# Joining the two moving operands of a split-precision product: 512 columns into one PSUM bank, halves added on VectorE

## What is computed

```
h = rms_norm(x, mix_norm_pre);  proj = h @ w_in          # then sparse attention, pooling, gating
x = x + rms_norm(mix @ w_out, mix_norm_post)
q = rms_norm(x) @ w_mq;  k = mem_n @ w_mk;  v = mem_n @ w_mv
x = x + rms_norm(attention(q, k, v) @ w_mo, mem_norm_post)
a = causal_conv3(rms_norm(x) @ w_up);  gate, val = split(a)
x = x + rms_norm((gelu(gate) * val) @ w_down, ffn_norm_post)
# second block, on 272 tokens: short-conv mixer, then mLSTM
q, k, v, o, z, g = split(u @ mlstm_in_w);  q = q * DK ** -0.5
out = rms_norm(x)[:, 16:]
```

## Time and profile before

| | us |
|---|---|
| median of 3 runs | 1003.33 (1000.75, 1003.33, 1003.83) |
| profiled execution, its own time | 1002.0 |
| its span, first to last instruction | 1000.3 |
| PE busy | 968.0 (97%), 7853 matmuls |
| VectorE busy | 676.6 (68%) |
| ScalarE busy | 545.8 (55%) |
| GpSimd busy | 135.0 (13%) |
| mean granted TensorE clock | 0.993 of full |

### The profile page before, as it was taken

How to read it: one execution, slowest core, us unless ns; L and a number is a source line. 1 busy time by engine, 2 the same in 40 slices (tenths; PEclk the granted TensorE clock), 3 DMA queues, 4 the chain that set the end, 5 groups by cost and what they waited for, 6 DMA issues and landing times. The chain is left out here.

```text
span 1000.3 us, 20837 instructions
## 1 busy us (share of the span) xinstructions
PE 968.0 (97%) x7853; PEld 928.2 (93%) x7853; DVE 676.6 (68%) x1048; ACT 545.8 (55%) x839; POOL 135.0 (13%) x137
## 2 busy tenths in 40 slices
PE   8998989999999999999999999999999999999997
PEld 7897769999899999998999999999999989999886
DVE  4878765654589988545877777766576447668843
ACT  6468456645499976554444434444453426654633
POOL 3003001001034455000111111101010000000000
PEclk9999989999999999999999999999999999999999
DMA  7743325435346655763455555555555433234551
GB/s 280 244 144 126 106 64 169 148 106 169 106 143 193 189 189 168 232 201 116 147 168 170 175 180 171 176 179 175 161 172 189 146 127 126 89 130 163 189 172 61
DMA packets 45176, 159.06 MB, mean 159 GB/s; under 512 B 6035, under 2 KB 7059, under 8 KB 44860
## 3 DMA queue, kind: packets, MB, share of 16 engines
q1 hardware_dynamic: 44668, 156.61, 48.9%
q0 software_dynamic: 448, 1.59, 0.6%
HBM read 157.11 MB, written 1.06 MB: 158 GB/s over the span
## 5 line engine op out<-in xcount | busy, mean ns | idle before, releaser
L1517 DVE TENSOR_TENSOR w_lo<-raw,w_hi 128x1024 fp32r<-128x1024 f32 x290 | 357.6, 1239 | 141.3 <-ACT w_hi L547 141.0
L547 ACT ACTIVATE w_hi<-raw 128x1024 fp32r<-128x1024 f32 x290 | 304.8, 1054 | 118.6 <-PE acc L1030 85.6
L1028 PE MATMUL acc<-AH,w_hi 128*128 128x256 f32 (+1 forms) x832 | 239.2, 287 | 0.9 <-DVE AL L1538 0.9
L1030 PE MATMUL acc<-AH,w_lo 128*128 128x256 f32 (+1 forms) x832 | 236.6, 284 | 0.0
L1029 PE MATMUL acc<-AL,w_hi 128*128 128x256 f32 (+1 forms) x832 | 236.4, 284 | 0.0
L1028 PE MATMUL acc<-XH,w_hi 128*128 128x256 f32 (+1 forms) x672 | 194.8, 290 | 8.7 <-DVE XL L1543 3.1
L1030 PE MATMUL acc<-XH,w_lo 128*128 128x256 f32 (+1 forms) x672 | 191.4, 285 | 0.0
L1029 PE MATMUL acc<-XL,w_hi 128*128 128x256 f32 (+1 forms) x672 | 191.2, 284 | 0.0
L1028 PEld LDWEIGHTS acc<-AH,w_hi 128*128 128x128 f32 x832 | 158.0, 190 | 2.7 <-issue 1.1
L1030 PEld LDWEIGHTS acc<-AH,w_lo 128*128 128x128 f32 x832 | 157.9, 190 | 0.0
L1029 PEld LDWEIGHTS acc<-AL,w_hi 128*128 128x128 f32 x832 | 157.7, 190 | 0.1
(11 more groups left out here) (357 smaller groups left out, 1404.1 us busy)
## 6 DMA issues: line engine op xcount, KB each, us to landing
raw<-weights SPq DMA_DIRECT2D x290, 512.0 KB, 3.5
cst<-params SPq DMA_DIRECT2D x1, 1195.0 KB, 13.4
XR<-x_t SPq DMA_DIRECT2D x2, 512.0 KB, 4.6
Y<-mem_t SPq DMA_DIRECT2D x1, 1024.0 KB, 10.8
AR<-bias_rows POOLq DMA_DIRECT2D x1, 1024.0 KB, 10.4
out<-AR SPq DMA_DIRECT2D x2, 512.0 KB, 3.0
AR<-final_gain POOLq DMA_DIRECT2D x1, 512.0 KB, 3.7
AR<-onehot SPq DMA_DIRECT2D x1, 66.0 KB
```

The costliest lines, as they stand in the source:

```text
L547: nc.scalar.activation(w_hi[:, n % SLOTS, :], raw[:, n % SLOTS, :], ACT.Copy).then_inc(hi_ready, 1)
L1028: nc.tensor.matmul(o, wh, h, start=start, stop=False)
L1030: return nc.tensor.matmul(o, wl, h, start=False, stop=stop)
L1517: V.tensor_tensor(w_lo[:, s, :], raw[:, s, :], w_hi[:, s, :].bitcast(F32), ALU.subtract).then_inc(lo_ready, 1)
```

## The change

High and low activations are laid into one tensor each (X2, M2, A2), so that one access pattern of 2 x 256 elements reads both. A new routine, `joined`, replaces `chunk`: per block one matmul of 512 moving columns (high and low) with w_hi into a whole bank, and one of 256 columns (high) with w_lo into its first half. It is used for all `mk` chunks, for tiles 0 to 6 of `w_out`, `mo` and `down`, for tiles 1 to 7 of `mq`, and for all of `lq`. The halves are added at evacuation by VectorE (`add_halves`, a reduction of 512 columns to 256). In `w_out`, `mo` and `down` the sum goes to Y, and ScalarE then waits for the evacuation, squares Y and scales it in place. GpSimd waits for `y_squared` in place of the evacuation. In `mq` a second instruction scales the sum, and the bank counts as free only after it. The factor S ** -0.5 moves from the evacuation of `lq` to that of `lk`.

```
-                    wait_chunk(act, n)
-                    nc.scalar.activation(Y[:, m, META:T], acc(t)[:, 0:S], ACT.Copy, scale=col(gain, m)).then_inc(y_ready, 1)
-                    freed(nc.scalar.activation(SQ[:, m, META:T], acc(t)[:, 0:S], ACT.Square), t)
+                    wait_evacuated(act, t)
+                    nc.scalar.activation(SQ[:, m, META:T], Y[:, m, META:T], ACT.Square).then_inc(y_squared, 1)
+                    nc.scalar.activation(Y[:, m, META:T], Y[:, m, META:T], ACT.Copy, scale=col(gain, m)).then_inc(y_ready, 1)
...
+            def joined(n, t, both, k0=0, nk=KT, total=KT, ready=None, order=None):
+                begin(n, t, k0 == 0)
+                o = acc(t)[:, :]
...
+                    nc.tensor.matmul(o.rearrange("p (a b) -> p a b", a=2), w_hi[:, s, cols], both(k),
+                                     start=(k0 == 0 and k == order[0]), stop=False)
+                    last = nc.tensor.matmul(o[:, 0:S], w_lo[:, s, cols], both(k)[:, 0, :], start=False,
+                                            stop=(k0 + nk == total and k == order[-1]))
+                last.then_inc(chunk_done, 1)
...
             for m in range(KT):
-                chunk(CHUNK["w_out"] + m, TILE["w_out"] + m, a_hi, a_lo, S, ready=mix_ready if m == 0 else None,
-                      order=(0, 1, 2, 4, 5, 6, 7, 3) if m == 0 else None)
+                if m < KT - 1:
+                    joined(CHUNK["w_out"] + m, TILE["w_out"] + m, a_parts, ready=mix_ready if m == 0 else None,
+                           order=(0, 1, 2, 4, 5, 6, 7, 3) if m == 0 else None)
+                else:
+                    chunk(CHUNK["w_out"] + m, TILE["w_out"] + m, a_hi, a_lo, S)
...
+            def add_halves(out, t):
+                return V.tensor_reduce(out, acc(t)[:, :].rearrange("p (a b) -> p b a", a=2), AX.X, ALU.add)
+
+            def join_y(name, m, n):
+                if m < KT - 1:
+                    wait_chunk(dve, n)
+                    freed(add_halves(Y[:, m, META:T], TILE[name] + m), TILE[name] + m)
...
-                        freed(V.tensor_copy(KTm[:, c, :], acc(t)[:, 0:S]), t)
+                        freed(add_halves(KTm[:, c, :], t), t)
...
             for m in range(KT):
                 ahead(CHUNK["w_out"] + m)
+                join_y("w_out", m, CHUNK["w_out"] + m)
...
-                freed(V.scalar_tensor_tensor(out=qM[:, m, :], in0=acc(t)[:, 0:S], scalar=(D // MEM_HEADS) ** -0.5, in1=rstd[:, META:T],
+                src = acc(t)[:, 0:S]
+                if m:
+                    src = qM[:, m, :]
+                    chain.link(add_halves(src, t))
+                freed(V.scalar_tensor_tensor(out=qM[:, m, :], in0=src, scalar=(D // MEM_HEADS) ** -0.5, in1=rstd[:, META:T],
...
             for c in range(24):
                 ahead(CHUNK["down"] + c)
+                if c % 3 == 2:
+                    join_y("down", c // 3, CHUNK["down"] + c)
...
-                freed(V.tensor_scalar(lq[:, m, :], acc(t)[:, 0:S], S ** -0.5, None, ALU.mult), t)
+                freed(add_halves(lq[:, m, :], t), t)
```

More of the change, by code:

```diff
@@ L137, in build @@
         XR = sb("XR", [P, KT, T])
[L138 to L143, removed]
+        X2 = sb("X2", [P, 2, KT, T], F32R)
+        M2 = sb("M2", [P, 2, KT, S], F32R)
+        A2 = sb("A2", [P, 2, E_TILES * T], F32R)
+        XH, XL = X2[:, 0, :, :], X2[:, 1, :, :]
+        MH, ML = M2[:, 0, :, :], M2[:, 1, :, :]
+        AH, AL = A2[:, 0, :], A2[:, 1, :]
         cst = sb("cst", [P, NCOLS])
@@ L299, in build @@
         rstd_ready = sem("rstd_ready")
-        y_ready, x_updated = sem("y_ready"), sem("x_updated")
+        y_ready, x_updated, y_squared = sem("y_ready"), sem("x_updated"), sem("y_squared")
         act_ready, act_hi, act_lo = sem("act_ready"), sem("act_hi"), sem("act_lo")
@@ L511, in _ @@
                         ffn_pool(p, 0, ffn_hi(p), ffn_lo(p))
-                sum_squares(lambda m: wait_evacuated(pool, TILE[name] + m), META)
+                sum_squares(lambda m: pool.wait_ge(y_squared, 7 * update + m + 1), META)
             with pool.Fori(0, E_TILES) as i:
@@ L1055, in chunk, with x_parts, m_parts, a_parts @@
                 last.then_inc(chunk_done, 1)
+            def joined(n, t, both, k0=0, nk=KT, total=KT, ready=None, order=None):
+                begin(n, t, k0 == 0)
+                o = acc(t)[:, :]
+                order = order or range(k0, k0 + nk)
+                s = n % SLOTS
+                for k in order:
+                    cols = slice((k - k0) * P, (k - k0 + 1) * P)
+                    if ready:
+                        ready(k)
+                    nc.tensor.matmul(o.rearrange("p (a b) -> p a b", a=2), w_hi[:, s, cols], both(k),
[3 more added lines that the diff above has]
+                last.then_inc(chunk_done, 1)
+            def x_parts(k):
+                return X2[:, :, k, META:T]
+            def m_parts(k):
+                return M2[:, :, k, :]
+            def a_parts(k):
+                return A2[:, :, span(k, S)]
+            def ffn_parts(k):
+                return a_parts(k) if k < 16 else m_parts(k - 16)
+            def l_parts(k):
+                return A2[:, :, (8 + k) * T + META:(9 + k) * T]
             def slots(part, n, cols):
@@ L1254, in _, with step_chunk @@
                     name, c = (("sgu_u", 0), ("pool", 0), ("mk", 0), ("mk", 2), ("mk", 4), ("mk", 6))[h - 1]
-                    x = (mem_h, mem_l) if name == "mk" else (xh, xl)
+                    def step_chunk(i):
+                        if name == "mk":
+                            joined(CHUNK[name] + c + i, TILE[name] + c + i, m_parts)
+                        else:
+                            chunk(CHUNK[name] + c + i, TILE[name] + c + i, xh, xl, S)
                     if h == 1:
@@ L1265, in _ @@
                         pe.wait_ge(mem_lo, 1)
-                    chunk(CHUNK[name] + c, TILE[name] + c, *x, S)
+                    step_chunk(0)
                     pv(h - 1)
-                    chunk(CHUNK[name] + c + 1, TILE[name] + c + 1, *x, S)
+                    step_chunk(1)
                 else:
@@ L1328, in _ @@
             for m in range(KT):
-                chunk(CHUNK["mq"] + m, TILE["mq"] + m, xh, xl, S, ready=raw_ready(RAW_X1) if m == 0 else None,
-                      between=(lambda: spread_rstd(NORM_X1, S)) if m == 0 else None)
+                if m == 0:
+                    chunk(CHUNK["mq"] + m, TILE["mq"] + m, xh, xl, S, ready=raw_ready(RAW_X1), between=lambda: spread_rstd(NORM_X1, S))
+                else:
+                    joined(CHUNK["mq"] + m, TILE["mq"] + m, x_parts)
                 if m == 2:
@@ L1350, in _ @@
             for m in range(KT):
-                chunk(CHUNK["mo"] + m, TILE["mo"] + m, a_hi, a_lo, S,
-                      ready=(lambda k: pe.wait_ge(act_lo, ACT_MEM + k // 2 + 1)) if m == 0 else None)
+                if m < KT - 1:
+                    joined(CHUNK["mo"] + m, TILE["mo"] + m, a_parts,
+                           ready=(lambda k: pe.wait_ge(act_lo, ACT_MEM + k // 2 + 1)) if m == 0 else None)
+                else:
+                    chunk(CHUNK["mo"] + m, TILE["mo"] + m, a_hi, a_lo, S)
             stat_y(NORM_MEMOUT, 2)
@@ L1368, in _ @@
                 for c in range(3):
-                    chunk(CHUNK["down"] + 3 * m + c, TILE["down"] + m, ffn_hi, ffn_lo, S, k0=8 * c,
-                          nk=min(8, FFN_TILES - 8 * c), total=FFN_TILES,
-                          ready=(lambda k: pe.wait_ge(act_lo, ACT_FFN + k + 1)) if m == 0 else None)
+                    n, t, nk = CHUNK["down"] + 3 * m + c, TILE["down"] + m, min(8, FFN_TILES - 8 * c)
+                    if m < KT - 1:
+                        joined(n, t, ffn_parts, 8 * c, nk, FFN_TILES,
+                               (lambda k: pe.wait_ge(act_lo, ACT_FFN + k + 1)) if m == 0 else None)
+                    else:
+                        chunk(n, t, ffn_hi, ffn_lo, S, k0=8 * c, nk=nk, total=FFN_TILES)
             stat_y(NORM_FFN, 3)
@@ L1395, in _ @@
             for m in range(KT):
-                chunk(CHUNK["lq"] + m, TILE["lq"] + m, l_in(AH, META), l_in(AL, META), S, ready=h1_ready if m == 0 else None)
+                joined(CHUNK["lq"] + m, TILE["lq"] + m, l_parts, ready=h1_ready if m == 0 else None)
                 if m == 5:
@@ L1870, in _ @@
                 ahead(CHUNK["mo"] + m)
+                join_y("mo", m, CHUNK["mo"] + m)
             post_norm(NORM_MEMOUT, 1, "g_ffn_pre", META)
@@ L1974, in lk_tiles @@
                     wait_chunk(dve, n)
-                    freed(V.tensor_tensor(lk[:, m, :], acc(t)[:, 0:T], rstd[:, :], ALU.mult), t)
+                    freed(V.scalar_tensor_tensor(out=lk[:, m, :], in0=acc(t)[:, 0:T], scalar=S ** -0.5, in1=rstd[:, :],
+                                                 op0=ALU.mult, op1=ALU.mult), t)
                     apply_norm(PRE_H1, "g_mlstm", 0, rstd[:, :], l_in(AH, 0), l_in(AL, 0), m)
```

2 lines of the change are left out of this document (added).

## The result

The changed kernel took **1014.36 us** (median of 4 runs, 1014.28 to 1014.59) against 1002.64 us of the kernel before (1000.75 to 1003.83, the three runs and the profiled execution together): ratio 1.0119, 95% interval 1.0102 to 1.0137. The forecast was slower, at 1010.1 us (1003 to 1015.5). The profiled execution took 1014.42 us, its span is 1012.7.

A forecast was written before the change was run, and what follows sets the result against it. The kernel was taken as bound by TensorE's matmul pace. Delays of 4.5, 4.3, 0.85, 0.35 and 0.06 less savings of 1.32, 0.55, 0.48 and 0.14 gave +7.6 us on 1002.0, thus 1009.6; forecast median 1010.1 us, range 1003 to 1015.5.

The forecast's parts named there:

- The loop: In w_out and mo, VectorE and ScalarE wait for each other, 3.67 us a turn against TensorE's 2.81: +4.5 and +4.3 us.
- The clock: Rival: the clock falls to half in the longer wait before stat_y, one or two stretches, 1012 to 1013.5 us; 15%.
- `mq`: Stage mq: 56 joined blocks save 0.48 us, the later end adds 0.85 us, net +0.4 us.
- the 0.85: At the end of mq, VectorE's reduction, link and scaling replace one 0.43 us instruction: +0.85 us.
- That is hidden in tiles 1 to 6, since banks are asked for a tile later: In mq, VectorE's longer evacuation of tiles 1 to 6 was to cost nothing; only the end would pay.
- the 0.0086 us: Saving per joined block, 0.3594 us before and 0.3508 after; 450 blocks, 3.9 us at most.
- `lq` and `lk`: Two reductions in lq's gate chain on VectorE, less slack: +0.35 us; the scaled evacuation of lk: +0.06 us.
- The 0.14 us of the last two chunks: In lq, the last two chunks were to give 0.14 us back.
- The rival of cheap weights: Rival: a 256-column matmul behind one of 512 comes down to 0.100 us, so 1004.4 us, no change to speak of; 7%.
- the one of 0.95 us: Rival: the reduction pays for its outputs, 0.95 us each, a turn of 3.94 us, 1014.7 us; 15%.
- the absorbing buffers: Rival: buffers absorb the loop in w_out and mo if a turn is at most 2.81 us; faster, about 1000.3 us; 7%.

The follow-up runs named there:

- The cut loop: Changed kernel with ScalarE's rounding of chunk m+4 moved ahead of tile m's square and scaled copy in w_out and mo: 1001.67 us, ratio 0.9996 to before.
- the two doses: Changed kernel, w_out and mo only: scaled copy moved behind the rounding, 1006.15 us; or VectorE's reduction replaced by a copy of 256 columns, 1009.62 us.
- the idle products: Changed kernel with idle TensorE products before the sum of squares in w_out and mo: 14 of them 1012.07 us, 7 of them 1011.91 us.
- the first half only: Changed kernel with VectorE's reduction in w_out and mo replaced by a copy of the bank's first 256 columns, some products left out: 1009.62 us.
- `mq` back: Changed kernel with mq as in the kernel before, all else joined: 1011.94 us in one execution.

## Why the prediction was right, and where it was short

**The loop** held, turn by turn. Forecast were a turn of 3.67 us, a reduction of 0.68, the square of `w_out` at 170.66 and +4.5 and +4.3 us. Measured are 3.66, 0.684, 170.70 and +4.36 and +4.10. That 170.70 falls on 170.66 is in part luck: the stage was entered 0.19 us later than in the trace from which I read the rows, and the last steps were 0.1 us shorter. And the row from which +4.5 was counted, 166.15, holds 0.46 us of a half-clock stretch; against the undisturbed 22.02 the loop cost 4.82 us in `w_out`. The cut loop gives all of it back, and the two doses give back 6 and 7 times what they take out. TensorE waits in front of the tiles, but 0.6 us and not 0.8 to 0.9, and from tile 4 on: the pace is 3.66 us a tile all the same. The rest of the difference is the latency of the last product before the wait (some 0.17 us, printed as busy) and a first product behind it that is 0.08 us slower.

**The clock** was priced right and given the wrong chance. "One or two stretches: 1012 to 1013.5" stood as a rival with 15%, for the case that came: +1.48 and +1.58 us, 3.1 in all, the larger part of the miss. The forecast left it out because the row it had was an idle time of 3.7 us, and the new waits are of 1.8 and 0.4 us. They were enough, in both stages of the profiled execution. That it was these waits is shown by the idle products: with the waits filled and the squares as late as before, the stretches are gone. In two kernels with a wait like them, it fell in one stage and not in the other: at 1.52 and not at 1.50 us, at 1.77 and not at 1.79 us. Where the wait was 1.4 us or filled it did not fall. The length of the wait alone does not decide: all ten traces have a wait of 1.49 or 1.50 us some 25 us behind the square of `mo` (at 280.64 us in the kernel before), and the clock fell behind it in none. What else decides is not shown here.

**`mq`** was the term that was wrong: forecast net +0.4, measured +1.26. The last tile cost 0.72 us of the 0.85: TensorE's idle time in front of L1340 is 0.85, but it was 0.13 already. The joined blocks gave 0.2 us here and not 0.48. The step that failed is "That is hidden in tiles 1 to 6, since banks are asked for a tile later". The banks were in time, but VectorE also produces the maxima for the softmax between these tiles, and one of them came 0.74 us later because of the reduction in front of it (2.21 us behind the start of the evacuation, for 1.47); TensorE's wait of 0.65 us for head 0 is not in the sum, nor 0.08 us of slower products behind it. 0.72 + 0.65 + 0.08 - 0.2 makes the 1.26.

**Columns.** Both prices that went into the 0.0086 us were read a little low. In the kernel before, the products of `mo` and `down` start 0.1200 us apart, and a block is 0.3600 and not 0.3594. The window of `down` in the earlier trace rows holds 5.8 us of the stage ahead of it, `up`, whose products of the same shape start 0.1183 us apart; `down` itself runs from 391.8 to 455 us, not from 384. Why the same shape has two paces no run here shows. After the change most blocks of `down` are 0.3533 us apart (88 blocks from 420.29 to 451.38): 0.2363 from the 512-column product to the next start and 0.1170 behind it. The sum of 0.2327, from the earlier trace rows, and 0.1200 is 0.3527, so the two runs of 256 in the moving operand cost nothing that shows; I had rounded the 0.2327 down to 0.231. That is 0.0067 us saved in a block, and 154 x 0.0067 is 1.03: `down` gave 1.04 for 1.32, `mk` 0.37 for 0.55. *TensorE: Matmul & The Clock Gate* of the Trainium skill (section "Back-to-back issue gap") gives N/2.4 + 2.5 ns as the gap of an isolated matmul, 2.5 ns for the start that is saved. The trace has 6.7 ns and does not agree; it lies between the rule and my 8.6.

**`lq` and `lk`**: +0.48 at the gate rows, for +0.41 (0.35 + 0.06). The 0.14 us of the last two chunks did not come: from the gate row to the end of the span it is 245.5 us in both kernels.

**Sum.** Against +7.6: clock +3.1, `mq` +0.9, smaller savings in `down` and `mk` +0.5, `lq` +0.2, an entry of `mk` that was 0.6 us later for reasons ahead of the change, and the loop -0.3: +12.4 in the profiled executions. So the mechanism of the forecast is the one that the runs show; 1010.1 missed 1014.36 by 4.3 us mostly for the clock, and the measured time lies inside the range because the range had been laid over that rival. The rival of cheap weights falls with the 0.1170 us behind a 512-column product (it needed 0.100), the one of 0.95 us with the 0.684, and the absorbing buffers with the turn of 3.66 us, where they needed 2.81.

## What to carry to other kernels

When work moves from one in-order engine to another that already follows it, write both orders side by side and look for a loop: A's instruction waits for B's, and behind it in A's queue stands what B's next one needs. What the turn is longer than the pace that it holds up (3.66 against 2.83 us here), times the turns, is the cost, whatever the busy shares say (ScalarE was at 54%, VectorE at 69%), and the cure is an order: what the other engine waits for goes ahead of what waits for the other engine. Give a new wait of 1.5 us or more on TensorE a real chance of a stretch at half clock behind it (4 of 6 here), and look at everything that is queued behind a lengthened evacuation, not only at its bank.

## What the hardware showed

- A reduction of 512 PSUM columns to 256 sums took 684 ns, as the one of 512 to 2 does (684 in the earlier trace rows); going from 2 outputs to 256 cost nothing that shows.
- The clock fell to half behind new waits of TensorE of 1.5 to 1.8 us in 4 of 6 cases: in both stages of the changed kernel, in one of two with the first half only and in one of two with `mq` back. It did not fall behind two waits of 1.4 us, nor behind the two that 7 idle products filled, nor behind a wait of 1.49 us that every kernel here has later in the program.
- What a stretch cost: 3.4 us at half clock cost 1.48 us behind `w_out` (1.5 again with the first half only) and 0.95 behind `mo` (6.23 for 5.28, with `mq` back), 6.8 us behind `mo` 1.58. The longer stretch was not the dearer one in proportion; that much of what stands there waits for other engines anyway is a guess.
- Matmuls of one shape, 128x256, started 0.1200 us apart in `mo` and `down` and 0.1183 us apart in `up`. A joined pair of 512 and 256 columns took 0.3533 us in most of `down` and 0.3466 in the first tiles of `w_out`.
